# One-hot rows of the coefficient stage moved from VectorE and ScalarE to GpSimd

## What is computed

```python
def one_block(xb):
    q = (xb @ w_q).reshape(PEER_BLOCK, PEER_HEADS, 2, PEER_DQ // 2)
    s = jnp.einsum("nhcd,hckd->nhck", q, sub_keys).astype(jnp.float32)
    v1, i1 = lax.top_k(s[:, :, 0], PEER_TOPK)
    v2, i2 = lax.top_k(s[:, :, 1], PEER_TOPK)
    ...
    gate = jax.nn.softmax(top_s, axis=-1)
    act = jax.nn.gelu(jnp.einsum("nd,nhkd->nhk", xb, u_tab[eidx]).astype(jnp.float32))
    coef = (gate * act).astype(xb.dtype)
    return jnp.einsum("nhk,nhkd->nd", coef, v_tab[eidx])
```

## Time and profile before

| | us |
|---|---|
| median of 3 runs | 3428.48 (3426.14 to 3432.98) |
| the profiled execution, its own time | 3431.14 |
| its span, first to last instruction | 3429.3 |
| VectorE's first instruction of the coefficient stage | 1341.22 |
| end of the last matmul of the stage | 1539.03 |

### The profile page before, as it was taken

The page is one execution under the profiler, slowest core; times in us unless marked ns, Lnnn a source line. Parts: engine busy times, 40 slices in busy tenths (PEclk is TensorE's granted clock), DMA queues, the critical chain, the costliest instruction groups (busy, mean ns, idle before and its releaser), DMA issues.

```text
span 3429.3 us, 46990 instructions
## 1 busy us (share of the span) xinstructions
PE 3072.3 (90%) x15879; PEld 2407.4 (70%) x15879; DVE 2569.0 (75%) x5749; ACT 794.6 (23%) x1610; POOL 1497.5 (44%) x1211
## 2 busy tenths in 40 slices
PE   5999539897999993776999999999999999999996
PEld 1465325543666663665888888888888888888885
DVE  2241880134478889996999999999999999999997
ACT  2101311201444444991111111111111111111112
POOL 0000000000075651005767776767667777676671
PEclk8899655698999997997999999999999999999998
DMA  8200010202788881679999999999999999999995
GB/s 335 105 1 0 2 14 1 115 0 98 298 336 332 321 323 47 188 201 363 394 395 392 391 393 388 394 391 391 392 390 393 389 397 390 392 391 394 391 391 221
DMA packets 321565, 954.95 MB, mean 278 GB/s; under 512 B 32642, under 2 KB 106370, under 8 KB 311442
## 3 DMA queue, kind: packets, MB, share of 16 engines
q0 software_dynamic: 147456, 536.94, 40.0%
q1 hardware_dynamic: 173988, 416.67, 33.1%
HBM read 837.72 MB, written 114.34 MB: 278 GB/s over the span
## 4 chain that ended last, share of the span: by engine, by line
PE 80%; DVE 7%; ACT 5%; DMA 4%; issue 3%; POOL 0%; ACTq 0%; SPq 0%; DVEq 0%
PE ps L854 28%; PE ps L843 23%; PE ps L731 7%; PE ps L710 4%; PE ps L602 3%; PE ps L754 2%; DMA arena<-in_w_ada 2%; PE ps L675 2%; DVE arena L1194 2%; PE ps L609 2%; PE ps L565 2%; ACT arena L1104 2%; ACT u_turn L1038 1%; ACT arena L1121 1%; PE ps L673 1%
## 5 line engine op out<-in xcount | busy, mean ns | idle before, releaser
L854 PE MATMUL ps<-w,v_rows 128*128 128x320 f32 (+1 forms) x4096 | 1033.9, 405 | 1.3 <-DVE y_sum L1194 1.3
L854 PEld LDWEIGHTS ps<-w,v_rows 128*128 128x128 f32 x4096 | 763.0, 190 | 204.8 <-DVE y_sum L1194 1.8
L528 POOL DMA_INDIRECT ring<-in_vt,arena x512 | 703.2, 1373 | 282.0 <-DVE y_rows L1703 187.6
L528 POOL DMA_INDIRECT ring<-u_table,arena x512 | 560.8, 1095 | 458.8 <-DVE ring L1689 214.1
L843 PE MATMUL ps<-h_hi,u_hi 128*128 128x320 f32 (+1 forms) x2048 | 654.7, 320 | 35.7 <-DVE u_lo L1194 33.9
L1703 DVE SCALAR_TENSOR_TENSOR y_rows<-ring,s5c,y_rows 128x1024 f32<-128x1024 f32 x512 | 652.1, 1274 | 9.9 <-DMA ring<-in_vt,arena 9.8
L1689 DVE SCALAR_TENSOR_TENSOR ring<-ring,h_rows 128x1024 f32<-128x1024 f32 x512 | 623.0, 1217 | 10.6 <-DMA ring<-u_table,arena 4.1
L843 PE MATMUL ps<-h_hi,u_lo 128*128 128x320 f32 (+1 forms) x2048 | 608.4, 297 | 0.0
L843 PE MATMUL ps<-h_lo,u_hi 128*128 128x320 f32 (+1 forms) x2048 | 608.3, 297 | 0.0
L493 POOL TENSOR_TENSOR arena<-arena 128x2048 f32<-128x2048 f32 (+1 forms) x28 | 73.2, 2633 | 1065.7 <-DVE arena L1194 1065.1
L843 PEld LDWEIGHTS ps<-h_hi,u_hi 128*128 128x128 f32 x2048 | 390.9, 191 | 42.9 <-DVE u_lo L1194 34.5
(11 more groups left out here) (231 smaller groups left out, 3179.5 us busy)
## 6 DMA issues: line engine op xcount, KB each, us to landing
u_turn<-in_ut SPq DMA_DIRECT2D x128, 512.0 KB, 6.9
u_table<-u_turn SPq DMA_DIRECT2D x128, 512.0 KB, 6.3
u_raw<-in_ut SPq DMA_DIRECT2D x128, 512.0 KB
v_rows<-in_vt SPq DMA_DIRECT2D x64, 1024.0 KB
coef_dram<-arena SPq DMA_DIRECT2D x9, 4096.0 KB, 16.3
c_raw<-coef_dram SPq DMA_DIRECT2D x64, 576.0 KB
arena<-in_w_ada SPq DMA_DIRECT2D x12, 2048.0 KB, 9.8
arena<-in_xp SPq DMA_DIRECT2D x2, 4096.0 KB, 21.5
```

The costliest lines, as they stand in the source:

```text
L528: nc.gpsimd.indirect_dma_start(out=slot(n), out_offset=None, in_=table, in_offset=bass.IndirectOffsetOnAxis(ap=uvi[:, at:at + 1], axis=0)) ...
L854: last = mm(ps[4 + m % 4][:, 0:width], seg(v_in_buf, 2048 * r + 1024 * e + P * d, P), seg(w_in_buf, ow, width), start=n == 0, stop=n == 3)
```

## The change

GpSimd makes the ungated one-hots of groups 0, 2, 4 and 6 of each block, ScalarE those of 1, 3 and 5, VectorE that of 7. GpSimd makes a group's rows in two steps: it subtracts (a TENSOR_TENSOR of 1024 columns), waits for itself, and compares the difference with zero in place (a TENSOR_SCALAR of 1024 columns). It keeps the same waits for free buffers as VectorE. TensorE waits for the engine that made the group's rows.

```diff
+POOL_GROUPS, ACT_GROUPS = (0, 2, 4, 6), (1, 3, 5)
...
+            def pool_rows(b, first):
+                for g in POOL_GROUPS:
+                    if not (first and g < 4):
+                        pool.wait_ge(s("c_full"), 8 * b + g - 3)
+                    shp = [P, 8, P]
+                    rows = ar(PQ + 2048 * (g % 4), 1024)
+                    nc.gpsimd.tensor_tensor(rows.rearrange("p (j n) -> p j n", j=8),
+                                            iota[:, :].unsqueeze(1).to_broadcast(shp),
+                                            itc(0, b, 8 * g, 8).unsqueeze(2).to_broadcast(shp),
+                                            ALU.subtract).then_inc(s("pool_rows_less"), 1)
+                    pool.wait_ge(s("pool_rows_less"), 4 * b + g // 2 + 1)
+                    nc.gpsimd.tensor_scalar(rows, rows, 0.0, None, ALU.is_equal).then_inc(s("pool_rows_ready"), 1)
+
             pool.wait_ge(s("picksT_moved"), 6)
+            pool.wait_ge(s("h_split"), 2)
+            pool_rows(0, True)
             u_rest(0)
+            for b in range(1, NB):
+                pool_rows(b, False)
...
-                    if g % 2:
-                        pe.wait_ge(s("i1_rows_ready"), 4 * b + g // 2 + 1)
+                    if g in ACT_GROUPS:
+                        pe.wait_ge(s("i1_rows_ready"), 3 * b + g // 2 + 1)
+                    elif g in POOL_GROUPS:
+                        pe.wait_ge(s("pool_rows_ready"), 4 * b + g // 2 + 1)
...
-                act.wait_ge(s("i1_squares_ready"), 4 * b + g // 2 + 1)
+                act.wait_ge(s("i1_squares_ready"), 3 * b + g // 2 + 1)
...
-                    if g % 2 and not (last and g > 3):
+                    if (g + 4) % 8 in ACT_GROUPS and not (last and g > 3):
                         first_rows(b + (g + 4) // 8, (g + 4) % 8)
...
-                    if g % 2 == 0:
+                    if g == 7:
                         tt(rows[:, 0], iota[:, :].unsqueeze(1).to_broadcast(shp),
                            itc(0, b, 8 * g, 8).unsqueeze(2).to_broadcast(shp), ALU.is_equal)
```

## The result

The changed kernel takes **3507.72 us** (median of 4 runs, 3505.41 to 3511.48) against 3430.39 us for the kernel before (median of 4): a ratio of 1.0228, 95% interval 1.0213 to 1.0243. It is slower by 77 us.

The account below looks back on a forecast made before the run. VectorE, stretched by GpSimd, was taken as the only bound: 162.0 us own work plus 148.0 us of holds make 310.0 us, ending the stage 114 us later; 3428.5 + 114.3 = 3543 us, range 3515 to 3586.

Parts of the forecast that it names:

- What bounds the kernel, and where the time goes: Coefficient stage: VectorE, held up by GpSimd, is the only bound; stage about 312 us in place of 198, later stages unchanged.
- the two classes that the prediction named: VectorE's one-hots in the coefficient stage: 0.33 us, and about 72 of them 2 to 3 us.
- its own sign of being wrong: Prediction wrong if full-length 0.33 us one-hots run during a GpSimd comparison, comparison far from 2.8 us, or stage under 200 us.
- I take the same loss for both instructions, because the one observed hold lasted the whole GpSimd instruction: GpSimd's difference and comparison each cost VectorE their length less 0.30 us: 4.11 us a group, 148.0 us for 36.
- The half-way case between the forecast and the first rival: GpSimd's comparison holds VectorE for only part of its length: time between 3453 us and the forecast; chance 0.03.
- the first rival: GpSimd's comparison does not hold VectorE, only the difference does: stage 25 us longer, 3453 us; chance 0.08.
- The difference: GpSimd's TENSOR_TENSOR of 1024 columns takes 1.93 us and costs VectorE that less 0.30 us.
- The remainder: GpSimd's 4.7 us for the first stream tile waits behind the first block's rows, costing nothing; its user comes 250 us later.
- The rule on the line rate: Skill's rate would give GpSimd's comparison 0.85 us, the sum 45 us in place of 114; prediction went by the trace rows.
- The rule on the shared way: VectorE instructions in a two-port mode and any GpSimd instruction exclude each other for the whole instruction; first come goes first.
- Side by side: Rival: engines run beside each other in the coefficient stage, which ends 13 us earlier: 3415 us; chance 0.04.
- More than the sum: Rival: TensorE at its lower clock stutters, GpSimd and VectorE wait for buffers, adding 36 us: 3579 us and above; chance 0.05.

## Why the prediction was right in kind and wrong in size

**What bounds the kernel, and where the time goes: right.** The stage alone got longer, VectorE sets its end, ScalarE and TensorE have slack, the stages behind it are unchanged. GpSimd's lengths were met to 3%. But the one-hots do not fall into the two classes that the prediction named: 440 last 0.33 us, 34 about 2 us (beside the differences) and 102 between 0.7 and 1.2 us (beside the comparisons). And its own sign of being wrong came: one-hots of 0.33 us run inside a comparison.

**The step that failed: "I take the same loss for both instructions, because the one observed hold lasted the whole GpSimd instruction".** The observed hold was that of a TENSOR_TENSOR; the comparison has one input and lets VectorE through in its middle. Its term was 2.48 us for a group and measured 1.33: 89.3 us were forecast, and the run with comparisons alone has 45.3, so 44 us too much. The half-way case between the forecast and the first rival was in the text, with 3 chances in 100; the row that would have given it more weight was the earlier trace rows, where the comparison needs 2.5 ns an element, half as much again as the difference, although it reads only one tensor, so that for part of its time it is likely to be neither reading nor writing.

**The difference: right.** 1.63 us forecast, 1.60 measured.

**The remainder: wrong in the other direction.** The text looked at who uses the remainder (the next stage) and not at what is queued behind it on GpSimd: the rows of the second block. In the kernel before that wait hurt nobody, since nothing stood behind it. It cost 14.3 us of VectorE's time and kept off holds of 11.3 us, by the run that moved it, the remainder's own 4.1 among them.

The sum, term by term, for VectorE's time in the stage: own work 157.9 us; differences 58.7 forecast, 54.5 by the run with them alone; comparisons 89.3 and 45.3; the remainder's hold 4.1 and 0; the gap 0 and 14.3. That is 310.0 forecast and 272.0 by the single runs, while the trace has 276.7 (1339.20 to 1615.85); the last 4.7 us are not taken apart. The gap, which the forecast did not have, made up for a part of the holds that it had too large: that it missed by no more than 35 us is in part luck.

**The rule on the line rate: rightly set aside.** The Trainium skill's "GPSIMD Engine Reference", section "4.1 Engine selection", would have a one-input instruction run at about the line rate; the comparison took 2.77 to 2.85 us for 1024 elements, and the measurement decides.

**The rule on the shared way: right about which forms, too strong about how long.** The Trainium skill's "SBUF — State Buffer", section "Who interferes with whom", names the plain tensor_scalar among the forms that can exclude GpSimd and leaves out the form that writes out its accumulator; the run with that form agrees (0.405 us at most, 2.08 in the plain form). Where that section of the Trainium skill says that the second to come is blocked for the whole instruction, the comparison differs, and the measurement decides: VectorE passed three one-hots in its middle.

**The rivals.** Comparison without a hold, 3453 us: it was right in that the comparison holds for less than its length, but it holds for 1.33 us; the measured 3508 us lies between this rival and the forecast. Side by side: excluded, 2.85 us for a group against the 0.94 from which it decides. More than the sum: the clock did fall, to 0.73 to 0.92 in the stretches shown, and cost nothing that shows, since VectorE was never idle in the stage outside the gap.

## What to carry to other kernels

An idle engine is not free capacity when its instructions hold up the engine that is the bound: first look for one place in the trace where the two already meet, and price each kind of instruction by its own meeting; what a two-input instruction does is no measure for a one-input one. The price of help is what it takes from the bound (here 2.9 us) against what it saves there (1.14 us), not what the helper needs. And when work is queued on an engine behind an old wait, that wait gets new victims.

## What was not expected of the hardware

A GpSimd TENSOR_SCALAR of 1024 columns held VectorE's plain one-hots in two pieces, about 1.0 us from its start and the last 0.9 us or so of its 2.8, in every comparison of the changed kernel that VectorE met from start to end, and in the same way where it did not write in place; as two instructions of 512 columns it cost VectorE 1.07 us in place of 1.33. And one form of VectorE's TENSOR_SCALAR was not held: with an accumulator written out, 576 of 576 ran undisturbed beside GpSimd (0.405 us at most), for a cycle of 0.327 us in place of 0.256.
